# Post-norm residual adds moved from VectorE to GpSimd in a two-block sequence model

## What is computed

```python
    for i in range(DEPTH):                      # DEPTH = 2
        g = norm_g[i]
        hn = rmsnorm(h, g[0])
        m = rwkv_pool_mixer(hn, ...) if i % 2 == 0 else diff_attn_mixer(hn, ...)
        h = h + rmsnorm(m, g[1])
        f = sq_relu_mlp(rmsnorm(h, g[2]), mlp_w1[i], mlp_w2[i])
        h = h + rmsnorm(f, g[3])
    return h[:, N_META:]
```

## Time and profile before

| what | value |
|---|---|
| time, median of 3 runs | 3115.97 us (3114.11 to 3116.03) |
| the profiled execution's own time | 3121.37 us |
| its span, first to last instruction | 3119.6 us |
| around the span | 1.8 us |
| TensorE busy / VectorE / ScalarE / GpSimd | 92% / 45% / 32% / 34% |
| mean granted TensorE clock | 0.965 |
| idle TensorE ahead of the first tile product, first two post-norms | 6.8 us each |

### The profile page before, as it was taken

How to read it: one execution, slowest core, us unless ns; L and a number is a source line. 1 busy time by engine, 2 the same in 40 slices (tenths; PEclk the granted TensorE clock), 3 DMA queues, 4 the chain that set the end, 5 groups by cost and what they waited for, 6 DMA issues and landing times.

```text
span 3119.6 us, 44776 instructions
## 1 busy us (share of the span) xinstructions
PE 2871.5 (92%) x17854; PEld 2346.1 (75%) x17854; DVE 1397.9 (45%) x2227; ACT 986.1 (32%) x1505; POOL 1067.7 (34%) x749
## 2 busy tenths in 40 slices
PE   6988989899899999998989888899998999899997
PEld 4666567677688578786778876799998866668885
DVE  5788364600206611302138574470634345293452
ACT  3222354222312236423225332312124454332221
POOL 0233122344324179444433410144442321234442
PEclk9999999999999999999999998999999998899999
DMA  3898111244572279322222100122222210122222
GB/s 134 260 259 268 69 41 48 78 135 161 154 211 98 95 182 262 104 95 74 88 86 68 36 3 22 61 94 89 88 94 74 78 42 20 54 81 94 95 94 74
DMA packets 130750, 324.85 MB, mean 104 GB/s; under 512 B 54145, under 2 KB 54785, under 8 KB 129809
## 3 DMA queue, kind: packets, MB, share of 16 engines
q1 hardware_dynamic: 96128, 221.90, 21.8%
q0 software_dynamic: 30096, 88.21, 10.2%
q10 hardware_dynamic: 4352, 12.26, 1.0%
HBM read 288.32 MB, written 33.95 MB: 103 GB/s over the span
## 4 chain that ended last, share of the span: by engine, by line
PE 69%; DVE 18%; DMA 4%; ACT 3%; issue 3%; POOL 3%; DVEq 1%; ACTq 0%; SPq 0%; POOLq 0%
PE ps L261 16%; PE ps L264 16%; PE ps L266 16%; PE ps L271 3%; DMA d_pb<-arena 3%; POOL ring_r L354 2%; DVE h L593 1%; PE ps L2829 1%; PE ps L915 1%; PE ps L1769 1%; PE ps L573 1%; PE ps L1510 1%; PE ps L1600 1%; PE ps L2180 1%; PE ps L2804 1%
## 5 line engine op out<-in xcount | busy, mean ns | idle before, releaser
L354 POOL TENSOR_TENSOR ring_r<-ring,high 128x1024 fp32r<-128x1024 f32 x327 | 815.5, 2494 | 1449.9 <-ACT high L363 1449.8
L261 PE MATMUL ps<-h_hi,high 128*128 128x512 f32 (+1 forms) x2104 | 735.1, 358 | 40.3 <-DVE ring_r L354 13.1
L266 PE MATMUL ps<-h_hi,ring_r 128*128 128x512 f32 (+1 forms) x2104 | 661.6, 349 | 0.0
L264 PE MATMUL ps<-h_r,high 128*128 128x512 f32 (+1 forms) x1912 | 643.1, 346 | 0.0
L363 ACT ACTIVATE high<-ring 128x1024 fp32r<-128x1024 f32 x359 | 379.5, 1057 | 822.8 <-PE ps L261 697.4
L261 PEld LDWEIGHTS ps<-h_hi,high 128*128 128x128 f32 x2104 | 399.6, 190 | 117.2 <-issue 48.9
L266 PEld LDWEIGHTS ps<-h_hi,ring_r 128*128 128x128 f32 x2104 | 369.8, 190 | 53.5
L264 PEld LDWEIGHTS ps<-h_r,high 128*128 128x128 f32 x1912 | 364.5, 191 | 41.6 <-issue 1.4
L264 PE MATMUL ps<-f_r,high 128*128 128x264 f32 (+1 forms) x832 | 261.2, 326 | 0.0
L261 PE MATMUL ps<-f_hi,high 128*128 128x264 f32 (+1 forms) x768 | 236.6, 321 | 0.0
L261 PE MATMUL ps<-z_hi,high 128*128 128x512 f32 x488 | 197.9, 405 | 29.7 <-POOL ring_r L354 23.9
(11 more groups left out here) (465 smaller groups left out, 4271.1 us busy)
## 6 DMA issues: line engine op xcount, KB each, us to landing
ring<-in_units SPq DMA_DIRECT2D x402, 512.0 KB, 3.2
d_ca<-arena POOLq DMA_DIRECT2D x16, 640.0 KB, 9.3
arena<-d_ca POOLq DMA_DIRECT2D x16, 640.0 KB, 5.7
arena<-d_q POOLq DMA_DIRECT2D x32, 256.0 KB, 8.3
d_pb<-arena POOLq DMA_DIRECT2D x16, 512.0 KB, 11.4
arena<-d_pb POOLq DMA_DIRECT2D x16, 512.0 KB, 4.1
arena<-d_ca POOLq DMA_DIRECT2D x16, 512.0 KB, 5.0
arena<-d_k POOLq DMA_DIRECT2D x128, 64.0 KB, 4.2
```

The lines of the kernel that those rows point to most:

```text
L261: part = mm(acc, hi[:, cols], self.x_hi(k)[:, t0:t0 + tn], start=(k == 0), stop=False)
L264: mm(acc, hi[:, cols], self.x(k)[:, t0:t0 + tn], start=False, stop=False)
L266: ins = mm(acc, w[:, cols], self.x_hi(k)[:, t0:t0 + tn], start=False, stop=(k == self.kt - 1))
L354: eng.tensor_tensor(b.ring_r[:, slot, :], b.ring[:, slot, :], self.high[:, (j + self.flip) % 2, :], ALU.subtract).then_inc(b.unit_lo, 1)
```

## The change

VectorE's loop loses the adds and the closing wait for them. `Rms` gets a GpSimd part that makes the eight adds, each when its normed tile is counted. Ahead of the adds GpSimd makes the low part of weight unit 1 of the following product (`led`), which was the first thing that the following product's own GpSimd part did; that part now starts at unit 2. The adds, their operands and their counts are the same. After the last post-norm `led` is empty.

```diff
@@ Gemm.gpsimd
             for j in range(self.body_units):
-                if not (self.late and isinstance(it, int) and it + j == 0):
+                if not (self.late and isinstance(it, int) and it == 0 and j < 2):
                     self.make_low(pool, j, it)
@@ Rms.__init__
         self.each = each
+        self.led = None
@@ Rms.vector
         for k in range(self.n + 2):
-            if self.onto and 1 <= k <= self.n:
-                dve.wait_ge(b.normed, at["ready"] + k)
-                b.nc.vector.tensor_tensor(self.onto(k - 1), self.onto(k - 1), self.out(k - 1),
-                                          ALU.add).then_inc(b.summed_onto, 1)
             if k < self.n:
                 b.nc.vector.scalar_tensor_tensor(
@@
-        if self.onto:
-            dve.wait_ge(*self.ready)
-
+
+    def gpsimd(self, pool):
+
+        if not self.onto:
+            return
+        if self.led:
+            self.led.low_unit(pool, 1)
+        for k in range(self.n):
+            pool.wait_ge(self.b.normed, self.at["ready"] + k + 1)
+            pool.tensor_tensor(self.onto(k), self.onto(k), self.out(k), ALU.add).then_inc(self.b.summed_onto, 1)
@@ LateRms.feed
-        gemm.between, self.gemm = self.between, gemm
+        gemm.between, self.gemm, self.before.led = self.between, gemm, gemm
@@ Turned.gpsimd
-        for u in range(1 if self.g.late else 0, self.tiles):
+        for u in range(2 if self.g.late else 0, self.tiles):
             self.g.low_unit(pool, u)
```

## The result

| | before | after |
|---|---|---|
| time, median of 12 runs each | 3114.79 us | 3127.45 us |
| ratio after / before, 95% interval | | 1.0038 (1.0029 to 1.0048) |
| profiled execution, own time | 3121.37 us | 3124.92 us |
| its span | 3119.6 us | 3123.1 us |

What follows compares the result with a forecast made beforehand. TensorE, busy 92%, bounds the kernel, so VectorE's post-norm chain matters only where TensorE waits. Terms 2.8 + 2.8 + 2.6 + 3.0 = 11.2 us on the median 3115.97 gave 3127.2; 8-in-10 range 3119.5 to 3137.

Steps and rivals of the forecast that it cites:

- The two engines exclude each other: In the post-norms: VectorE instructions with two SBUF inputs and GpSimd's adds block each other, but for 0.22 us per GpSimd instruction.
- A turn of 1.78: First post-norm: one normed tile (0.69) plus one GpSimd add (1.09) alternate at 1.78 us, eighth add at 15.09 against 11.47.
- 0.8 given back behind it: Behind the eighth residual tile, first post-norm: one subtraction is already done, so work up to the square sums comes 0.8 us earlier.
- The second place: Second post-norm: same shape as the first, net +2.8 us; earlier table and weight loads counted as nothing beyond the 0.8.
- The unit moved ahead costs nothing: Low part of weight unit 1, ahead of the adds: runs on an idle GpSimd before the first normed tile, 0 us.
- long after: Low parts of unit 2 on: queued behind GpSimd's new waits but only asked for long after, costed at nothing.
- The last place, +3.0: Last post-norm: no subtractions follow, eighth add at 14.2 against 11.19 us, output transfers following each add as before.
- three terms: Net cost of the first three post-norms: +2.8, +2.8 and +2.6 us.
- Overlap: Rival, all post-norms: GpSimd's adds run beside VectorE's tiles and set the pace; -5.8 us, 3110; chance 0.09.
- kept out: Rival, all post-norms: GpSimd waits until VectorE's stream of normed tiles ends; +17.9 us, 3134; chance 0.26.
- a short add: Rival, all post-norms: GpSimd's add takes 1.06 us instead of 1.27; +4.4 us, 3120.4; chance 0.08.
- a longer clock dip: Rival, three places: TensorE's half-speed clock lasts through half of the second output; 9 us more, 3136; chance 0.07.

## Why the prediction was right, step by step

- **The two engines exclude each other**, read off four normed tiles and one subtraction elsewhere in the program. Right, and shown by moving one operand to PSUM.
- **A turn of 1.78.** It was 1.73 (the adds of the first place end 14.71 after the first normed tile; forecast 15.09). The overlap of an add with the next normed tile is nearer 0.27 than the 0.22 taken from the earlier trace rows, six times in a row. With 512 columns it was 1.67 instead of 1.72. The eighth add came +3.24 later instead of +3.6.
- **0.8 given back behind it.** 3.24 - 2.46 = 0.8. The reason given was right as well: one subtraction is done by then, and GpSimd's low part of unit 2 takes 2.69 instead of 3.49. TensorE's wait for the square sums fell from 1.45 to 1.08.
- **The second place** without more given back: +2.37, like the first. The earlier table loads did remove TensorE's wait for unit 2's low part, 1.08 in the kernel before and absent after, but as forecast the square sums behind it ended as in the first place.

```profile
2406.26 0.39 PE L261 MATMUL ps<-h_hi,high 128*128 128x264 f32 x1 [1.08 <-POOL ring_r L354]
```

- **The unit moved ahead costs nothing.** True of what it costs. What it is worth, 2.35 a place, I had no number for; "long after" for the units behind it was right.
- **The last place, +3.0.** This step failed. The turns were right (eighth add at 13.76; forecast 14.2), but "the output transfers follow each add as before" ended the sum too early. GpSimd's closing drain, which ends 5.56 us after its last instruction, was in the trace of the kernel before, covered by 22 us of other engines' work. The prediction did not list it even among the things costed at nothing; giving the last eight instructions to an engine that had been idle took the drain's cover away. It cost 3.3 to 3.4 in the profiles.
- **The total** came out near the forecast (11.8 against 11.2) with the places' sum at 13.0: three terms 0.3 to 0.4 too high, one 2.9 too low. The interval of the timing (9.0 to 15.0) holds all of these. So the closeness of the total is in part luck: errors of opposite sign met, and the mechanism was complete in three places of four.
- **The rivals.** Overlap, kept out, a short add and a longer clock dip all fell: the turns are in every profile of the changed order, and the adds took 1.25 undisturbed. (The kept-out rival's four terms add up to 18.2, not to the 17.9 given; nothing hangs on it.) The row on which kept out rested was moreover the second time that GpSimd asked in the middle of that stream of VectorE subtractions. The first time it got in at once, and it was the next subtraction that was held, recorded at 2.87 us instead of 0.68:

```profile
1452.80 2.44 POOL L354 TENSOR_TENSOR ring_r<-ring,high 128x1024 fp32r<-128x1024 f32 x1 [2.76 <-ACT high L363]
```

- **TensorE's clock** was the nearest rival: the low level lasted longer than before, but was over well ahead of the second output at 2006.8, as the busy time by stretch shows (the clock is the third number from the right; half speed is the 1.2 GHz level). Counted from the first normed tile the full level is back by 7 us in the kernel before (first row) and by 9.5 us in the changed one (the other two):

```profile
1998.00:2000.00 2.00, 2.00 (x9) 1.50 (x9) 1.93 (x4) 1.85 (x4) 0.00 (x0) 0.92 0.63 234
```

```profile
1996.00:1998.00 2.00, 2.00 (x6) 1.54 (x5) 2.00 (x2) 1.39 (x3) 2.00 (x2) 0.50 0.75 252
...
2000.00:2002.00 2.00, 1.58 (x6) 0.68 (x5) 2.00 (x2) 1.50 (x3) 2.00 (x3) 1.00 0.00 0
```

What stays open: what kept GpSimd out for 6 us in the earlier trace rows. It is no property of a gapless stream as such (the normed tiles are one, and 7.5 us earlier in the same stream it was let in at once), nor of satisfied waits (tested), and with the weight unit behind the adds it was let in between two subtractions. Yet at the step from the last subtraction to the first square sum it was passed over once in the kernel before (the 3.49 of the earlier trace rows) and in the third place too.

## What to carry to other kernels

Moving the elementwise adds from VectorE to GpSimd relieved nothing here while VectorE's neighbouring instructions read two tensors from SBUF: each pair then costs the sum of the two (0.69 + 1.04, against 1.43 for both on VectorE). With one of VectorE's operands in PSUM the engines run side by side, and a part of the adds on GpSimd gained 2.5 us by the places, which twelve timed runs do not yet tell from nothing; all eight adds on GpSimd still did not pay in the last place, because of the drain. And look at what an engine does *after* its last instruction before giving it the last work of a program: GpSimd needed 5.56 us to reach the end, so its last instruction should lie that far ahead of it.

## What was not expected of the hardware

- GpSimd's closing `DRAIN` ends 5.54 to 5.56 us after its last instruction in all twelve profiles, whether that was a subtraction of 128x1024, an add of 128x512 or a copy of 128x1.
- With one operand in PSUM VectorE's two-tensor instruction is not slower (0.753 median against 0.756), and a reciprocal written to PSUM took the same 3.46 us as one to SBUF.
- Whole-program times of the kernel before scatter by 10 us in twelve runs and by 17 in the 32 of another series, while most post-norms repeat within about 0.1; stretches between fixed landmarks resolved differences of 0.8 us a place that twelve timed runs did not.
